# Encoder block with a 32-expert MoE: the expert loop rewritten, with the gate half computed one expert ahead

## The reference, cut to what matters

```
D_MODEL = 1024; SEQ = 512; N_EXPERTS = 32; TOP_K = 4; D_FF = 1024

def clamped_swiglu(gu):
    gate, up = gu[..., :D_FF], gu[..., D_FF:]
    gate = jnp.minimum(gate, 7.0)
    up = jnp.clip(up, -7.0, 7.0)
    return (up + 1.0) * (gate * jax.nn.sigmoid(1.702 * gate))

def moe(h, w_router, b_router, w_gate_up, b_gate_up, w_down, b_down):
    logits = h @ w_router + b_router
    top_vals, top_idx = lax.top_k(logits, TOP_K)      # 4 of 32 experts for each token
    gate = jax.nn.softmax(top_vals, axis=-1)
    # the tokens of each expert e are gathered (xb), and for them:
    gu = xb @ w_gate_up[e] + b_gate_up[e]             # 1024 -> 2048
    y = clamped_swiglu(gu) @ w_down[e] + b_down[e]    # 1024 -> 1024
    # y * gate is added to the rows of its tokens

x = x + merged @ w_out                                # end of attention
x = x + moe(rmsnorm(x, g_ffn), ...)
return rmsnorm(x, g_final)
```

## Time and profile before

| | |
|---|---|
| median of three runs | 1695.3 us |
| span of the profiled execution, first to last instruction | 1694.0 us |
| TensorE busy | 1615.0 us (95%) |
| VectorE busy | 1378.4 us (81%) |
| ScalarE busy | 1053.7 us (62%) |
| GpSimd busy | 225.3 us (13%) |
| mean granted TensorE clock | 0.981 of full speed |
| first expert matmul | at 480.79 us |
| last expert matmul | at 1671.74 us |

### The profile page before, as it was taken

The page is one execution under the profiler, slowest core; times in us unless marked ns, Lnnn a source line. Parts: engine busy times, 40 slices in busy tenths (PEclk is TensorE's granted clock), DMA queues, the critical chain, the costliest instruction groups (busy, mean ns, idle before and its releaser), DMA issues.

```text
span 1694.0 us, 23640 instructions
## 1 busy us (share of the span) xinstructions
PE 1615.0 (95%) x7535; PEld 1162.2 (69%) x7535; DVE 1378.4 (81%) x1477; ACT 1053.7 (62%) x1039; POOL 225.3 (13%) x111
## 2 busy tenths in 40 slices
PE   7999899999869999999999999999999999999994
PEld 6788555678747677777777777777777776777773
DVE  4365464545589999999999999999999999999994
ACT  4243343422446777677777777777777777777763
POOL 6400000000001112111111211111121111111210
PEclk9999799999979999999999999999999999999997
DMA  8322000004589999999999999999999999999983
GB/s 278 114 100 75 16 1 1 1 26 174 193 304 337 357 360 361 356 348 370 360 365 357 364 347 360 360 362 366 359 362 351 356 365 359 360 366 361 352 301 121
DMA packets 177565, 466.86 MB, mean 276 GB/s; under 512 B 9688, under 2 KB 10208, under 8 KB 161056
## 3 DMA queue, kind: packets, MB, share of 16 engines
q1 hardware_dynamic: 166032, 432.63, 70.3%
q0 software_dynamic: 7904, 28.12, 7.0%
q10 hardware_dynamic: 3600, 5.73, 1.0%
HBM read 446.19 MB, written 20.25 MB: 275 GB/s over the span
## 4 chain that ended last, share of the span: by engine, by line
PE 91%; DVE 4%; ACT 2%; DMA 1%; issue 1%; ACTq 0%; SPq 0%; DVEq 0%; POOLq 0%
PE ps L1121 26%; PE ps L1123 26%; PE ps L1122 26%; PE ps L1216 2%; PE ps L1192 2%; PE ps L1229 2%; PE ps L1373 2%; PE ps L1399 2%; PE ps L1196 1%; DVE hidT L1024 1%; PE ps L1236 1%; ACT hidT L682 1%; PE ps L1405 1%; DVE mx L820 1%; DVE split L761 1%
## 5 line engine op out<-in xcount | busy, mean ns | idle before, releaser
L957 DVE TENSOR_TENSOR split<-raw,split 128x2048 fp32r<-128x2048 f32 x384 | 866.2, 2285 | 29.8 <-ACT split L624 26.5
L624 ACT ACTIVATE split<-raw 128x2048 fp32r (+1 forms) x384 | 714.3, 1909 | 12.3 <-PE ps L1123 10.2
L1121 PE MATMUL ps<-split,XT 128*96 128x512 f32 x1024 | 413.3, 404 | 4.7 <-DVE XT L1017 4.7
L1123 PE MATMUL ps<-split,XT 128*96 128x512 f32 x1024 | 403.8, 394 | 0.0
L1122 PE MATMUL ps<-split,XT 128*96 128x512 f32 x1024 | 401.2, 392 | 0.0
L466 POOL DMA_INDIRECT sum_rows<-y,idx x32 | 101.4, 3169 | 1013.5 <-ACT y L718 1013.5
L1121 PE MATMUL ps<-split,hidT 128*96 128x512 f32 x512 | 210.0, 410 | 9.4 <-DVE hidT L1024 9.4
L1121 PEld LDWEIGHTS ps<-split,XT 128*96 128x96 f32 x1024 | 166.9, 163 | 71.7 <-issue 4.9
L1123 PEld LDWEIGHTS ps<-split,XT 128*96 128x96 f32 x1024 | 165.2, 161 | 72.2
L1122 PEld LDWEIGHTS ps<-split,XT 128*96 128x96 f32 x1024 | 166.0, 162 | 67.0
L1123 PE MATMUL ps<-split,hidT 128*96 128x512 f32 x512 | 201.4, 393 | 0.0
(11 more groups left out here) (241 smaller groups left out, 2031.8 us busy)
## 6 DMA issues: line engine op xcount, KB each, us to landing
raw<-in_w_gate_up SPq DMA_DIRECT2D x256, 1024.0 KB, 10.8
raw<-in_w_down SPq DMA_DIRECT2D x128, 1024.0 KB, 5.7
raw<-in_w_in SPq DMA_DIRECT2D x14, 1024.0 KB, 6.6
w_out<-in_w_out SPq DMA_DIRECT2D x4, 1024.0 KB, 6.1
xs<-in_x SPq DMA_DIRECT2D x4, 512.0 KB, 5.3
raw<-in_w_branch_a SPq DMA_DIRECT2D x2, 1024.0 KB, 5.1
raw<-in_w_branch_b SPq DMA_DIRECT2D x2, 1024.0 KB, 5.1
sum_rows<-xs ACTq DMA_DIRECT2D x4, 512.0 KB, 2.6
```

The source lines that it names most:

```text
L624: a.activation(split[:, s % NSPLIT, 0, :], raw_slot(i, s), ACT.Copy).then_inc(ex_hi, 1)
L957: v.tensor_tensor(split[:, s % NSPLIT, 1, :], raw_slot(i, s), split[:, s % NSPLIT, 0, :].bitcast(F32), ALU.subtract).then_inc(ex_lo, 1)
L1121: mm(dst, lhsT(0), rhs(0), start=start, stop=False)
L1123: return mm(dst, lhsT(1), rhs(0), start=False, stop=stop)
```

## The change

The expert loop is rewritten in all engines; nothing ahead of the router changes but constants.

- Order on TensorE: an item's gate product (4 chunks) is computed inside the item before it, between that one's up and down products. Item 0's gate product stands ahead of the loop, and the last item stands behind the loop, without a gate part.
- `hidden_T` is one block of eight transposes in the middle of the next item's gate product, and `rows_in` stands in the middle of the up product.
- At the end of an item TensorE waits until its own last chunk's matmuls have completed, and then raises a semaphore (`down_ps`) for ScalarE's y.
- Chunks are 256 rows x 1024 columns (rows of 4 KB in memory), in 12 fixed places; lo is written over the raw chunk, hi into a ring of 6. A place is free when TensorE has used the chunk.
- SwiGLU is three VectorE passes over 96x1024: sigmoid from PSUM on ScalarE, then gate x sigmoid, clamp of up (the bias has the 1 in it), and minimum and product in one.
- The row indices are computed by five small ScalarE operations; `serve` on VectorE is one operation; y is one operation of 96x1024.

```
# TensorE
+            def pe_item(i, nxt):
+                for c in range(4, 8):
+                    if c == 6:
+                        if nxt:
+                            rows_in(i + 2)
+                        else: ...
+                    weigh(order(i, c, nxt), c, hi_slot(c, nxt), XT, 2, True)
+                pe.wait_ge(sel_ready, i + 1)
+                add_bias(2, 1, False).then_inc(up_ps, 1)
+                pe.wait_ge(y_ready, i + 1)
+                add_bias(4, 2, True).then_inc(down_begun, 1)
+                if nxt:
+                    pe.wait_ge(glu_ready, i + 1)
+                    for c in range(4):
+                        if c == 0:
+                            pe.wait_ge(xt_lo, 2 * i + 3)
+                        weigh(order(i, c, nxt), c, hi_slot(c, nxt), XT, 0, True)
+                        if c == 0:
+                            slots(i + 3)
+                        if c == 1:
+                            pe.wait_ge(f5_ready, i + 4)
+                            pe.wait_ge(xt_lo, 2 * i + 4)
+                            hidden_T(i + 1)
+                    pe.wait_ge(sel_ready, i + 2)
+                    add_bias(0, 0, False).then_inc(gate_ps, 1)
+                else:
+                    hidden_T(i + 1)
+                pe.wait_ge(hidT_lo, i + 1)
+                for c in range(8, 12):
+                    last = weigh(order(i, c, nxt), c, hi_slot(c, nxt), hidT, 4, False)
+                pe.wait_ge(ex_used, order(i, 11, nxt) + 3)
+                pe.sem_inc(down_ps, 1)
+            with pe.Fori(0, last_item) as i:
+                pe_item(i, True)
+            pe_item(last_item, False)
# ScalarE
             def act_item(i, nxt):
                 if nxt:
+                    for c in range(3):
+                        ex_split_hi(i + 1, c)
+                    rows_hi(i + 2, 0)
+                    ex_split_hi(i + 1, 3)
+                ex_split_hi(i, 8, nxt)
                 if nxt:
+                    act.wait_ge(ex_used, 12 * i + 10)
+                    rows_hi(i + 2, 1)
+                ex_split_hi(i, 9, nxt)
                 if nxt:
+                    act.wait_ge(scattered, 16 * i + ADDED)
+                    index(i + 3, bass.ds((i + 3) % 4, 1))
+                ex_split_hi(i, 10, nxt)
+                hidden_hi(i + 1)
+                ex_split_hi(i, 11, nxt)
+                if nxt:
+                    a.activation(warm[:, :], eps[:, :], ACT.Sigmoid)
+                    sigmoid(i + 2)
+                    for c in range(4, 8):
+                        ex_split_hi(i + 1, c)
...
+                act.wait_ge(down_ps, i + 1)
...
# VectorE
             def dve_item(i, nxt):
+                    serve(i + 3)
+                    for c in range(3):
+                        ex_split_lo(i + 1, c)
+                    rows_lo(i + 2, 0)
+                    ex_split_lo(i + 1, 3)
+                dve.wait_ge(up_ps, i + 1)
+                v.tensor_scalar(hid, ps[0:CAP, 2:4, :]..., 8.0, -6.0, ALU.min, ALU.max)
...
+                v.scalar_tensor_tensor(out=hid, in0=sg, scalar=SILU_TOP, in1=hid, op0=ALU.min,
+                                       op1=ALU.mult).then_inc(hid_ready, 1)
                 if nxt:
+                    choose_bias((i + 1) % E)
+                    rows_lo(i + 2, 1)
+                ex_split_lo(i, 8, nxt)
+                ex_split_lo(i, 9, nxt)
+                hidden_lo(i + 1)
+                ex_split_lo(i, 10, nxt)
                 if nxt:
+                    glu(i + 2)
+                ex_split_lo(i, 11, nxt)
+                if nxt:
+                    for c in range(4, 8):
+                        ex_split_lo(i + 1, c)
# SP, ahead of the loop: chunks 4 to 7 and 8 to 11 of expert 0 without a wait for a place
             sp.wait_ge(wout_ps, 2 * NT)
+            for c in range(4, 8):
+                load_expert(sp, c, 0)
             sp.wait_ge(scattered, ADDED)
             sp.dma_start(bias_tab[0:96, :], bias_parts).then_inc(bias_back, 16)
+            for c in range(8, 12):
+                load_expert(sp, c, 0)
```

More of the change, by code:

```diff
@@ L285, in blocks, with expert_src, load_expert, order @@
             return t.rearrange("p (k n) -> p k n", n=width)
[L289 to L309, removed]
+        def expert_src(e, c):
+            q = c % 4
+            if c < 8:
+                w = w_gate_up[0, e, q * 256:(q + 1) * 256, (c // 4) * FF:(c // 4 + 1) * FF]
+            else:
+                w = w_down[0, e, q * 256:(q + 1) * 256, :]
+            return w.rearrange("(p k) n -> p k n", k=2)
+        def load_expert(sp, c, e):
+            sp.dma_start(chunk[c][:, :].rearrange("p (k n) -> p k n", k=2), expert_src(e, c)).then_inc(expert_in[c], 16)
+        def order(i, c, nxt):
+            q = c - 4 if c in range(4, 8) else c + 4 if c < 4 else c if nxt else c - 4
+            return 12 * i + 4 + q
+        def hi_slot(c, nxt=True, first=False):
+            if first:
+                return c
+            q = c - 4 if c in range(4, 8) else c + 4 if c < 4 else c if nxt else c - 4
+            return (4 + q) % NHI
+        def expert_w(c, h, part, k, t):
+            at = k * 1024 + t * 512
+            return (chunk_hi[h] if part == 0 else chunk_lo[c])[:, at:at + 512]
         def window(n):
@@ L665, in _ @@
+            index(0, slice(0, 1))
+            act.wait_ge(gates_set, 1)
+            first_split_hi(3)
+            index(1, slice(1, 2))
+            act.wait_ge(gates_set, 2)
             act.wait_ge(logits_ps, NT)
-            ex_split_hi(0, 2)
-            ex_split_hi(0, 3)
+            index(2, slice(2, 3))
+            rows_hi(1, 0)
+            rows_hi(1, 1)
             act.wait_ge(rows_stored, 2 * NT * 16)
[L669 to L678, removed]
@@ L1041, in _ @@
             v.tensor_copy(items_i[:, 0:1], npass[:, :]).then_inc(items_ready, 1)
+            dve.wait_ge(idx_done, 1)
+            serve(1)
+            choose_bias(0)
+            for c in range(1, 3):
+                ex_split_lo(0, c, first=True)
+            dve.wait_ge(idx_done, 2)
+            serve(2)
+            ex_split_lo(0, 3, first=True)
+            rows_lo(1, 0)
+            rows_lo(1, 1)
             dve.wait_ge(items_ready, 1)
             last_item = dve.value_load(items_i[0:1, 1:2], min_val=E - 1, max_val=E * PASSES - 1)
-            base = steps[0] - 3
@@ new lines, in hidden_T, with weigh @@
+            def hidden_T(n):
+                pe.wait_ge(hid_ready, n)
+                for k in range(KD):
+                    last = t_.transpose(ps[:, 6 + k // 4, (k % 4) * CAP:(k % 4 + 1) * CAP],
+                                        hid[:, (k // 2) * 256 + k % 2:(k // 2 + 1) * 256:2], ident[0:CAP, 0:CAP])
+                last.then_inc(hidT_ps, 1)
+            def weigh(at, c, h, src, bank, fresh):
+                pe.wait_ge(ex_lo, at + 1)
+                q = c % 4
+                for k in range(2):
+                    for t in range(2):
+                        last = mm_split(ps[0:CAP, bank + t, :], lambda p: src[:, p, 2 * q + k, :],
+                                        lambda p: expert_w(c, h, p, k, t),
+                                        start=(fresh and q == 0 and k == 0), stop=(not fresh and q == 3 and k == 1))
+                last.then_inc(ex_used, 1)
+                return last
@@ new lines, in add_bias @@
+            def add_bias(bank, part, start):
+                for t in range(2):
+                    col = part * FF + t * 512
+                    last = mm(ps[0:CAP, bank + t, :], sel[:, :], bias_tab[0:96, col:col + 512], start=start, stop=not start)
+                return last
+            slots(0)
+            slots(1)
+            slots(2)
+            pe.wait_ge(f5_ready, 3)
+            rows_in(1)
+            pe.wait_ge(xt_lo, 2)
+            for c in range(4):
+                weigh(c, c, c, XT, 0, True)
```

412 lines of the change are left out of this document (169 added, 243 removed).

## The result

The changed kernel takes 1714.9 us, median of 4 runs (1713.8 to 1722.5), beside 1696.1 us for the kernel before (4 runs; 1695.3 is the median of three of them). The ratio is 1.0123, with a 95% interval of 1.0103 to 1.0143: slower by 1.2%. The profiled execution has a span of 1713.3 us, 19.3 more than before. The runs of several of these kernels fall into two groups some 7 us apart (here three at 1713.8 to 1715.1 and one at 1722.5), so where a few us matter the lowest run of one is set beside the lowest of the other.

What follows compares the result with a forecast made beforehand. The prediction took TensorE to be the bound. From a span of 1694.0, loop +18.6, start -1.3 and both ends +5.4 gave 1716.7 us, and with 1.3 from span to median 1718; range 1700 to 1732.

Steps and rivals of the forecast that it cites:

- What bounds the kernel: In the expert loop, TensorE at its own pitch is the bound; VectorE has some 1.9 us of slack per item.
- The wait at the item's end, +0.95 us: TensorE waiting for its own last chunk: 0.46 lost, 0.44 for the loop's own instructions, 0.04 for a register operation.
- Rival B: Item's end: the wait costs its 0.46, the loop's own instructions nothing on top; median 1702.8; chance 0.12.
- Rival A: Loop: the wait at the item's end costs nothing, so the change is faster; median 1688.5; chance 0.09.
- The wait for the hidden values and the transposes, -0.45 and +0.10: TensorE, per item: the wait for hidden values goes, -0.45 us; 16 transposes go by a dearer row, +0.1 us.
- The covers: New order within an item: VectorE, ScalarE and DMA results all come before TensorE needs them; least slack 3.2 us.
- Rival C: Loop: VectorE becomes the bound, later by 4 us than reckoned; each further 1 us is 31, then 1749; chance 0.07.
- D: Loop code on TensorE's queue is fetched again each round; at 2 us, 62 us more, 1780; chance 0.02.
- The start, -1.3 us: Start of the experts: first product sooner with VectorE free, but a loaded gather takes 9.4 us; between -2.7 and 0.
- Both ends, +5.4 us: Pipeline ends: first gate product 13.3 and last item 31.0, together 44.3 where one item of 38.9 was.
- The range: Whole time: 1700 to 1732, which takes in B and leaves out A, D and most of C.
- main case: The forecast without the rivals: 1718, alone running from 1709 to 1727; chance 0.70.

Runs made afterwards that it cites:

- e1: The changed kernel without TensorE's wait for its own last chunk and without down_ps; ScalarE's y waits for ex_used itself: 1690.8 us, ratio 0.9971.
- e4: The changed kernel with three more VectorE passes over 96x512 in each item behind the SwiGLU product: 1715.9 us.
- e9: The changed kernel with every weight chunk loaded by two transfers of 512 columns, rows read 2 KB at a time: 1717.6 us.
- e3: As e1, with TensorE's wait for its own matmuls put back in the middle of the down product: 1704.3 us, ratio 1.0057.
- e7: As e1, but in the last item VectorE writes the hidden lo ahead of the split of chunk 9: 1684.8 us, ratio 0.9942.
- e6: As e1, but SP loads chunks 8 to 11 of expert 0 only when the first gather has landed: 1684.3 us, ratio 0.9932.
- e8: As e1, with both the late load of chunks 8 to 11 (e6) and the last item's order (e7): 1680.3 us, ratio 0.9904.
- e5: The kernel before with one more GpSimd operation (96x1024, adds 0) heading the bias chain: 1691.6 to 1692.1 us for seven of ten runs, ratio 0.999.
- e11: As e1, with VectorE's splits of expert 0's chunks 1 to 3 behind its lo of the first gathered rows: 1681.2 us, ratio 0.9923.
- e12: As e8, with VectorE's splits behind the first gather as in e11: 1679.1 us, ratio 0.9908.
- e10: As e8, without the three subtractions in GpSimd's chain for the bias parts (low parts come out wrong): 1680.3 us.

## Why the prediction was right, and where its sum was off

1718 was forecast, 1714.9 measured. The forecast's claim was that a rewrite which spares VectorE some 6% of its work in the loop gains nothing, and that one wait of two lines decides. That claim held for the reason given. That the number is only 3 us off is in part luck: of the span's 22.7 us the loop came out 7.2 lower, the start 2.5 and the two ends 1.7 higher. By its own steps:

*What bounds the kernel.* Shown. TensorE at its own pitch is the bound: in e1 it is busy 36.62 of an item's 36.62 us, e4 and e9 changed nothing, e1 and e3 moved the time by what they did to TensorE's sequence.

*The wait at the item's end, +0.95 us.* Measured 0.92 (after against e1), made of 0.53 and 0.39 (e3) where the sum had 0.46 and 0.49. Rival B, no cost for the loop's own instructions, falls by the 0.39. Rival A falls too, yet e1 is about what it would have been: 1687.0 in the lower group of its runs for A's 1688.5.

*The wait for the hidden values and the transposes, -0.45 and +0.10.* Together measured as 36.61 - 37.17 = -0.56 (e1 against before), for -0.35. This is the mis-sized term. The changed order has two places of eight transposes each; this is one:

```profile
1002.72 1.08 PE L1399 MATMUL ps<-ident,hid 96*128 96x96 f32 x8
...
1003.58 0.45 PE L1164 MATMUL ps<-chunk_hi,XT 128*96 128x512 f32 x1
```

From the first transpose to the next product it is 0.86, so the product follows the last transpose by 0.07 where the sum had allowed 0.12. By that the removed wait was worth 0.51 (before, the last transpose started at 1033.94 and the product at 1034.51, 0.58 apart), and the start behind it came after 0.31 where it is 0.29 behind the other groups: 0.53 in all. The 0.10 for the transposes isn't there: 16 of them take 2 x 0.86 = 1.72 us by the starts, and before it was the same 1.72 without the wait. It is 31 x 0.2 = 6 us, most of what the loop came out below the forecast: 31 x 0.37 = 11.4 us for 18.6. The covers' own list of times, which ends at 36.5 before the wait of 0.95, came nearer (36.61 and 37.54) than the sum of differences (37.8), and the two were not set against each other.

*The covers.* All held: VectorE made the product in time, hidden lo waited for ScalarE only, DMA kept up. VectorE was busy 32.7 an item for the 33.1 reckoned, though the sum took 26.6 for the twelve splits where the earlier trace rows has 27.1. Rival C had nothing in the trace, and D neither: the page has 19 blocks on the instruction queue q8, one more than before. That q8 is TensorE's was taken, the page doesn't say so; its packets in the changed kernel's trace start at 480.0, 513.0 and then 1663.3 us, none between: whosever they are, nothing was loaded there in rounds 2 to 31 of the loop.

*The start, -1.3 us.* Measured +1.2 (482.01 against 480.79), as the sum of three things, none of them sized rightly: the gather was issued 3.7 us sooner; VectorE's queue ahead of XT's lo was shorter by 3.1, for 2.7; and the gather's rows took 14.9 us instead of 6.9, for 9.4 forecast. I had taken a loaded gather's 9.4 from the earlier trace rows, and left out what VectorE's splits do to GpSimd.

*Both ends, +5.4 us.* From the first expert product to the last matmul it is 1209.4 us, for 1190.9 before: 18.5, less the loop's 11.4 leaves 7.1. The stall in the last item was 8.1 (from 1671.0, where the up bias is done by the starts, to 1679.08), for 8.35 reckoned. What the sum hadn't is the clock: the last down product took 12.6 for 11.1, and the first gate product 13.9 for 13.3.

```profile
1670.57 1.03 PE L1419 MATMUL ps<-bias_tab,sel 96*96 96x512 bf16 x4
...
1673.73 1.20 PE L1399 MATMUL ps<-ident,hid 96*128 96x96 f32 x8 [2.14 <-DVE hid L1126]
...
1679.08 0.74 PE L1164 MATMUL ps<-chunk_hi,hidT 128*96 128x512 f32 x1 [4.15 <-DVE hidT L1074]
1679.62 0.63 PE L1165 MATMUL ps<-chunk_lo,hidT 128*96 128x512 f32 x1
1680.04 0.63 PE L1166 MATMUL ps<-chunk_hi,hidT 128*96 128x512 f32 x1
```

The first seven pitches of the last down product are 0.54 and then 0.43 or 0.41, after TensorE had two gaps of 2.1 and 4.2 us; the granted clock from 1679.08 to 1682 is 0.50 of full speed, the level of 1.2 GHz. Together they are 3.1 us where the pitch of 0.23 makes 1.6: 1.5 us. The first gate product starts with 13 such pitches, where item 0 of the kernel before has nine; that is the other 0.6.

In sum: 11.4 + 7.1 + 1.2 - 0.3 behind the last matmul = 19.4 of span, for the 22.7 forecast.

*The range.* Its main case was given as from 1709, "end of item 0.76, start -2.7"; by its own terms that is 1718 - 31 x 0.19 - 1.4 = 1710.7, and 1707.6 with no cost for the transposes.

## What to carry to other kernels

When TensorE is the bound, never let its program wait for its own matmuls, least of all just ahead of a loop's branch: let the engine that needs their result wait on the semaphore that the last matmul raises (e1). A wait inserted to signal someone else costs its queue (0.5 us) and everything that its sequencer had been doing ahead (0.4 us), per item. That is this kernel's price, measured in two orders of one loop. And where three engines look full, ask what was waited for, and check a named releaser against its own times, before you spare an engine work.

## What the runs showed of the hardware

**VectorE's splits and GpSimd hold each other up.** In the projection stage GpSimd's subtractions (6.1 us, 32x3072) run beside VectorE's splits. VectorE and GpSimd in the changed kernel's profiled run:

```profile
42.45 2.29 DVE L827 TENSOR_TENSOR split<-raw,split 128x2048 fp32r<-128x2048 f32 x1 [11.52 <-ACT split L531]
45.59 7.22 DVE L827 TENSOR_TENSOR split<-raw,split 128x2048 fp32r<-128x2048 f32 x1 [0.85 <-ACT split L531]
```

```profile
42.57 8.10 POOL L468 TENSOR_TENSOR bias<-bias,bias_new 32x3072 f32<-32x3072 f32 x1
50.73 4.69 POOL L469 CAST bias_new<-bias 32x3072 bf16<-32x3072 f32 x1
```

And the same two in e7's:

```profile
43.26 12.84 DVE L827 TENSOR_TENSOR split<-raw,split 128x2048 fp32r<-128x2048 f32 x2 [11.73 <-ACT split L531]
```

```profile
43.16 6.04 POOL L468 TENSOR_TENSOR bias<-bias,bias_new 32x3072 f32<-32x3072 f32 x1
49.27 4.69 POOL L469 CAST bias_new<-bias 32x3072 bf16<-32x3072 f32 x1
```

In the first the split began 0.1 us ahead of the subtraction and took 2.29, and only the next was caught: it began at 45.59, the subtraction ended at 50.67, and the split ended 2.1 us behind that, 7.2 us after its start. In the second the subtraction began 0.1 us ahead: two splits were caught and took 12.8. The subtraction in its turn took 8.10 us in the first and 6.04 in the second. The 200th matmul starts at 59.4 in the one and at 66.3 in the other. The other profiled runs agree: in e6 and e8 (1689.1 and 1687.1 us, well above their lowest) the subtraction began first and the 200th matmul starts at 66.0 and 65.1; in e1, e3, e4, e5, e9, e11 and e12 the split began first and it starts between 58.7 and 59.9. So this accounts for the 7 us between the two groups, as far as runs were profiled. e10, without the subtractions, has no long splits, and no second group either, but four runs prove little there (e8 has one of four in it).

It goes the other way too: the first gather's issue on GpSimd took 7.14 us beside splits and 1.02 without. Not every gather pays that: in the loop, where VectorE splits most of the time, the median issue is 2.4 us in the changed kernel and 2.29, the length of a split, in the kernel before. What decides between 2.3 and 7.1 no run here shows.

**The clock is low behind the long gaps and not behind the short one.** Behind TensorE's last idle stretches (6.6 and 4.7 us at the start of the kernel before, 2.1 and 4.2 in the last item of the changed kernel) the granted clock is about 0.5 of full speed (0.52 from 480.79 to 484.79, and 0.50 from 1679.08 to 1682), and nine and seven starts follow each other by some 0.43 us before the pitch is 0.23 again. The gap of 0.7 us at the end of each item left the granted clock at 1.00.
